# Six weight slots behind each layer's end taken by parts: first parts per half of the tokens, second parts last, GpSimd's rounding behind the norm

## The reference

```python
for i in range(2):                                   # first_block
    h = rms_norm(x, ln_mix_pre[i])
    m = gla_mixer(h, ...) if i == 0 else swa_sink_mixer(h, ...)
    x = x + rms_norm(m, ln_mix_post[i])
    h = rms_norm(x, ln_mlp_pre[i])
    f = jnp.square(jax.nn.relu(h @ w_up)) @ w_down
    x = x + rms_norm(f, ln_mlp_post[i])
for l in range(2):                                   # second_block
    h = even_mixer(x, ...) if l == 0 else odd_mixer(x, ...)
    x = layer_norm(ALPHA * x + h, ln_mix_g[l], ln_mix_b[l])
    x = layer_norm(ALPHA * x + swiglu(x, ...), ln_ffn_g[l], ln_ffn_b[l])
```

## Time and profile before

| | us |
|---|---|
| median of 3 runs | 2440.15 (2439.74 to 2441.57) |
| the profiled execution | 2440.48 |
| its span in the profile | 2438.6 |
| PE busy | 2380.8 (98% of the span) |
| POOL busy | 1095.1 (45%) |
| ACT busy | 933.6 (38%) |
| DVE busy | 706.0 (29%) |

### The profile page before, as it was taken

One profiled execution on the slowest core, in us unless ns is written; L12 is line 12 of the kernel. 1 busy time (PEld: TensorE's weight loads), 2 busy tenths in 40 slices (PEclk: granted clock), 3 DMA queues, 4 the chain that ended last, 5 costly groups with the idle time before them and its releaser, 6 DMA issues.

```text
span 2438.6 us, 29746 instructions
## 1 busy us (share of the span) xinstructions
PE 2380.8 (98%) x11723; PEld 1958.7 (80%) x11723; DVE 706.0 (29%) x1160; ACT 933.6 (38%) x1872; POOL 1095.1 (45%) x899
## 2 busy tenths in 40 slices
PE   8999999999989999999999999999999999999998
PEld 7867888888867888887887788888888768888887
DVE  2223430122454420223254541101152374110103
ACT  4523442433474442433254423323333572332331
POOL 4523544454433554444354444444445503444443
PEclk9999999999999999999999999999999999999999
DMA  5312233332312333322231233333333302333332
GB/s 177 87 51 67 87 96 98 93 100 82 87 35 70 94 97 96 97 97 82 83 108 61 69 96 104 97 96 97 100 95 82 96 1 80 116 100 95 95 100 74
DMA packets 161330, 215.59 MB, mean 88 GB/s; under 512 B 38175, under 2 KB 86039, under 8 KB 161191
## 3 DMA queue, kind: packets, MB, share of 16 engines
q1 hardware_dynamic: 157632, 203.65, 27.8%
q10 hardware_dynamic: 3559, 10.04, 1.2%
HBM read 211.00 MB, written 2.10 MB: 87 GB/s over the span
## 4 chain that ended last, share of the span: by engine, by line
PE 91%; DVE 5%; POOL 2%; issue 1%; ACT 1%; DMA 0%; ACTq 0%; DVEq 0%; POOLq 0%
PE PS L333 15%; PE PS L334 14%; PE PS L335 14%; PE PS L339 13%; PE PS L341 13%; PE PS L340 13%; PE PS L1393 1%; PE PS L1375 1%; PE PS L414 1%; PE PS L2191 1%; POOL WL L306 1%; DVE X L654 1%; PE PS L993 1%; PE PS L2178 0%; DVE X L536 0%
## 5 line engine op out<-in xcount | busy, mean ns | idle before, releaser
L306 POOL TENSOR_TENSOR WL<-WS,WH 128x512 fp32r<-128x512 f32 (+2 forms) x788 | 1005.4, 1283 | 1132.0 <-ACT WH L299 1127.8
L299 ACT ACTIVATE WH<-WS 128x512 fp32r<-128x512 f32 (+2 forms) x788 | 479.5, 615 | 1240.5 <-PE PS L341 626.7
L333 PE MATMUL PS<-AH,WH 128*128 128x512 f32 (+1 forms) x1712 | 641.0, 374 | 4.4 <-DVE AL L449 3.2
L334 PE MATMUL PS<-AL,WH 128*128 128x512 f32 (+1 forms) x1712 | 637.8, 373 | 0.0
L335 PE MATMUL PS<-AH,WL 128*128 128x512 f32 (+1 forms) x1712 | 637.7, 372 | 0.0
L333 PEld LDWEIGHTS PS<-AH,WH 128*128 128x128 f32 x1712 | 324.9, 190 | 62.7 <-issue 5.4
L335 PEld LDWEIGHTS PS<-AH,WL 128*128 128x128 f32 x1712 | 324.8, 190 | 56.0
L334 PEld LDWEIGHTS PS<-AL,WH 128*128 128x128 f32 x1712 | 324.9, 190 | 55.4 <-issue 0.5
L341 PE MATMUL PS<-WH,h_HL 128*128 128x512 f32 x864 | 336.1, 389 | 0.0
L339 PE MATMUL PS<-WH,h_HH 128*128 128x512 f32 x864 | 336.1, 389 | 0.0
L340 PE MATMUL PS<-WL,h_HH 128*128 128x512 f32 x864 | 336.1, 389 | 0.0
(11 more groups left out here) (320 smaller groups left out, 1887.5 us busy)
## 6 DMA issues: line engine op xcount, KB each, us to landing
WS<-in_mlp_w_up_dram SPq DMA_DIRECT2D x128, 256.0 KB, 2.8
WS<-in_mlp_w_down_dram SPq DMA_DIRECT2D x128, 256.0 KB, 2.6
WS<-in_ffn_w_gate_dram SPq DMA_DIRECT2D x176, 128.0 KB, 2.1
WS<-in_ffn_w_up_dram SPq DMA_DIRECT2D x176, 128.0 KB, 2.2
WS<-in_ffn_w_down_dram SPq DMA_DIRECT2D x88, 256.0 KB, 2.6
WS<-in_gla_w_in_dram SPq DMA_DIRECT2D x48, 256.0 KB, 2.7
WS<-in_even_w_in_dram SPq DMA_DIRECT2D x48, 256.0 KB, 2.7
WS<-in_odd_w_in_dram SPq DMA_DIRECT2D x32, 256.0 KB, 2.7
```

The source lines that it names most:

```text
L299: e.activation(WH[:, s, 0:n], WS[:, s, 0:n], ACT.Copy).then_inc(hi.sem, hi.tick(i))
L306: e.tensor_tensor(WL[:, s, 0:n], WS[:, s, 0:n], WH[:, s, 0:n].bitcast(F32), ALU.subtract).then_inc(lo.sem, lo.tick(i))
L333: e.matmul(o, h, xh[:, cs], start=start, stop=False, skip_group_check=free)
L334: e.matmul(o, h, xl[:, cs], start=False, stop=False, skip_group_check=free)
```

## The change

In a head PE now takes first parts of the weights only, for pieces 0 to 3 and then 4 and 5: all matmuls `AH` by `WH`, then all `AL` by `WH`. The transposes of the second half stand between the halves. The matmuls with `WL` follow behind both halves, all tokens at once. POOL makes the six second parts behind the last tile's norm, for which it waits. ACT and DVE take the features of the first half one bank at a time between their other work. The layer norm's variance of tile 3 is taken ahead of the features.

```diff
-                for half in range(2):
-                    for kc in range(HEAD):
-                        if half == 0 and kc == HEAD - 1:
-                            head()
-                        w.wait_ge(lo, i0 + kc)
-                        for at in ready(kc, half):
-                            w.wait_ge(*at)
...
-                            q = three(kc, m, cs)
-                        if half == 1:
-                            q.then_inc(mm.sem, mm.tick("used", i0 + kc))
+                for half in range(2):
+                    if half:
+                        head()
+                    cs = slice(256 * half, 256 * half + 256) if kind == "F" else slice(0, T)
+                    ms = range(count(0)) if kind == "F" else (2 * half, 2 * half + 1)
+                    for kcs in (range(HEAD - 2), range(HEAD - 2, HEAD)):
+                        for kc in kcs:
+                            w.wait_ge(hi, i0 + kc)
+                            for at in ready(kc, half, False):
+                                w.wait_ge(*at)
+                            for m in ms:
...
+                                one(kc, m, WH, xs[kc][0], cs, start=kc == 0 and (kind == "T" or half == 0))
+                        for kc in kcs:
+                            for at in ready(kc, half):
+                                w.wait_ge(*at)
+                            for m in ms:
+                                one(kc, m, WH, xs[kc][1], cs)
+                for kc in range(HEAD):
+                    w.wait_ge(lo, i0 + kc)
+                    for m in range(count(kc)):
+                        q = one(kc, m, WL, xs[kc][0])
+                    q.then_inc(mm.sem, mm.tick("used", i0 + kc))
@@ act_rms_close
-            run(weight_steps(weight_hi, e, w, name + ".1", nk, nk - TAIL))
+            late = weight_steps(weight_hi, e, w, name + ".1", nk, nk - TAIL)
+            for _ in range(4):
+                next(late)
+            act_feat(e, w, name, 0, BA, gain, free, [0])
             act_put(e, w, name, 3, 1, BA[3], other)
-            act_feat(e, w, name, 0, BA, gain, free, range(2))
+            act_feat(e, w, name, 0, BA, gain, free, [1])
             sumsq(2)
-            act_feat(e, w, name, 0, BA, gain, free, range(2, 4))
             sumsq(3)
+            next(late)
+            act_feat(e, w, name, 0, BA, gain, free, [2])
+            run(late)
+            act_feat(e, w, name, 0, BA, gain, free, [3])
@@ dve_rms_close
-            dve_feat(e, w, name, 0, BA, gain, free, range(2))
+            dve_feat(e, w, name, 0, BA, gain, free, [0])
             dve_add(e, w, name, 3)
-            dve_feat(e, w, name, 0, BA, gain, free, range(2, 4))
+            dve_feat(e, w, name, 0, BA, gain, free, [1])
             if normed:
                 dve_norm_mid(e, w, name, 2)
                 dve_norm_out(e, w, name, 2)
                 dve_norm_mid(e, w, name, 3)
                 dve_norm_out(e, w, name, 3)
+            dve_feat(e, w, name, 0, BA, gain, free, range(2, 4))
@@ pool_rms_close
-            late = weight_steps(weight_lo, e, w, name + ".1", nk, nk - TAIL)
-            for _ in range(3):
-                next(late)
             pool_rstd(e, w, name, 3)
-            next(late)
             if normed:
                 pool_norm_mid(e, w, name, 2)
-            run(late)
-            if normed:
                 pool_norm_mid(e, w, name, 3)
+            w.wait_ge(ve, "hn" if normed else "x", name, 3)
+            run(weight_steps(weight_lo, e, w, name + ".1", nk, nk - TAIL))
@@ dve_ln_close
             dve_ln_put(e, w, name, 3, 1, b1[3], scale)
+            dve_ln_var(e, w, name, 3)
             if not last:
-                dve_feat(e, w, name, 0, b1, None, free)
+                dve_feat(e, w, name, 0, b1, None, free, range(2))
             dve_ln_out(e, w, name, 2, b_)
-            dve_ln_mean(e, w, name, 3, g, gtok)
+            dve_ln_centre(e, w, name, 3, g, gtok)
+            if not last:
+                dve_feat(e, w, name, 0, b1, None, free, [2])
             dve_ln_out(e, w, name, 3, b_)
+            if not last:
+                dve_feat(e, w, name, 0, b1, None, free, [3])
@@ pool_ln_close
-            for t in range(3):
+            for t in range(4):
                 pool_ln_rstd(e, w, name, t)
-            late = weight_steps(weight_lo, e, w, name + ".1", nk, nk - TAIL)
-            for _ in range(5):
-                next(late)
-            pool_ln_rstd(e, w, name, 3)
-            run(late)
+            w.wait_ge(ve, "x", name, 3)
+            run(weight_steps(weight_lo, e, w, name + ".1", nk, nk - TAIL))
```

More of the change, by code:

```diff
@@ L324, in gemm, with one, three @@
             i0 = first[name]
-            def three(kc, m, cs=slice(0, T)):
-                s, n, (xh, xl), b = (i0 + kc) % NS, width(i0 + kc), xs[kc], banks[m]
-                last, start = kc == nk - 1, kc == 0 and cs.start == 0
-                free = head is not None
+            def one(kc, m, weight, x, cs=slice(0, T), start=False, stop=False):
+                s, n, b = (i0 + kc) % NS, width(i0 + kc), banks[m]
                 if kind == "F":
-                    h, l = WH[:, s, m * mw:(m + 1) * mw], WL[:, s, m * mw:(m + 1) * mw]
-                    o = PS[b][0:mw, cs]
-                    e.matmul(o, h, xh[:, cs], start=start, stop=False, skip_group_check=free)
-                    e.matmul(o, h, xl[:, cs], start=False, stop=False, skip_group_check=free)
-                    return e.matmul(o, l, xh[:, cs], start=False, stop=last, skip_group_check=free)
-                h, l = WH[:, s, 0:n], WL[:, s, 0:n]
-                o = PS[b][:, 0:n]
-                ts = slice(m * P, (m + 1) * P)
-                e.matmul(o, xh[:, ts], h, start=start, stop=False, skip_group_check=free)
-                e.matmul(o, xh[:, ts], l, start=False, stop=False, skip_group_check=free)
-                return e.matmul(o, xl[:, ts], h, start=False, stop=last, skip_group_check=free)
+                    return e.matmul(PS[b][0:mw, cs], weight[:, s, m * mw:(m + 1) * mw], x[:, cs], start=start, stop=stop,
+                                    skip_group_check=head is not None)
+                return e.matmul(PS[b][:, 0:n], x[:, m * P:(m + 1) * P], weight[:, s, 0:n], start=start, stop=stop,
+                                skip_group_check=head is not None)
+            def three(kc, m):
+                xh, xl = xs[kc]
+                one(kc, m, WH, xh, start=kc == 0)
+                if kind == "F":
+                    one(kc, m, WH, xl)
+                    return one(kc, m, WL, xh, stop=kc == nk - 1)
+                one(kc, m, WL, xh)
+                return one(kc, m, WH, xl, stop=kc == nk - 1)
             def count(kc):
@@ L350, in gemm @@
                 for half in range(2):
-                    for kc in range(HEAD):
-                        if half == 0 and kc == HEAD - 1:
-                            head()
-                        w.wait_ge(lo, i0 + kc)
-                        for at in ready(kc, half):
-                            w.wait_ge(*at)
-                        ms = range(count(kc)) if kind == "F" else (2 * half, 2 * half + 1)
-                        for m in ms:
-                            if kc == 0 and held.get(banks[m]):
-                                w.wait_ge(*held[banks[m]])
-                            cs = slice(256 * half, 256 * half + 256) if kind == "F" else slice(0, T)
-                            q = three(kc, m, cs)
-                        if half == 1:
-                            q.then_inc(mm.sem, mm.tick("used", i0 + kc))
+                    if half:
[8 more added lines that the diff above has]
+                            for m in ms:
+                                if kc == 0 and held.get(banks[m]):
+                                    w.wait_ge(*held[banks[m]])
+                                one(kc, m, WH, xs[kc][0], cs, start=kc == 0 and (kind == "T" or half == 0))
[9 more added lines that the diff above has]
+                    q.then_inc(mm.sem, mm.tick("used", i0 + kc))
                 yield HEAD - 1
@@ L453, in feats @@
         def feats(name):
-            return lambda kc, half: [(ve, "feat", name, half, kc)]
+            return lambda kc, half, rest=True: [(ve, "feat", name, half, kc) if rest else (sc, "feat", name, half, kc // 2)]
         def act_sumsq(e, w, name, t):
@@ L1249, in pool_gla @@
                 pool_norm_mid(e, w, "n0", t)
+            for t in range(2, 4):
+                pool_norm_mid(e, w, "n0", t)
+            w.wait_ge(ve, "hn", "n0", 3)
             for i in range(NS):
                 weight_lo(e, w, i)
-            for t in range(2, 4):
-                pool_norm_mid(e, w, "n0", t)
             run(weight_steps(weight_lo, e, w, "gla.q", 8))
```

25 lines of the change are left out of this document (17 added, 8 removed).

## The result

| | before, us | changed, us |
|---|---|---|
| median | 2440.82 (2439.74 to 2441.57, 4 runs) | 2422.40 (2419.45 to 2424.84, 4 runs) |
| ratio | | 0.9924, 95% interval 0.9907 to 0.9942 |
| span of the profiled execution | 2438.6 | 2423.0 |

The change takes 18.4 us off the median (0.76%); the forecast was 18.1, at 2422.0. The changed kernel was timed again in three later experiments: 2422.53, 2420.90 and 2421.63, ratios 0.9925, 0.9911 and 0.9925, each with an interval of some 0.0013 to either side.

The account below looks back on a forecast made before the run. PE, busy 98% of the span, bounds the kernel, with idle time to win only at layers' ends behind DVE's norms and features. Nine heads' wins sum to 18.1 us: 2440.15 - 18.1 = 2422.0, forecast range 2417 to 2427.

Parts of the forecast that it names:

- the sum: All nine heads: wins from earlier second transposes, less what goes behind them, add up to 18.1 us.
- swa.q0 and mlp1: Heads behind mlp0 and at mlp1: second transposes at 9.9 instead of 14.6 at swa.q0; wins 3.6 and 3.3 us.
- What is paid behind the second transposes: Every head: matmuls moved behind cost 1.1 us in kind F, 1.4 in kind T, 0.8 at odd.
- mlp0: Head at mlp0: transposes end 4.3 behind the last matmul, half done at 11.4; win 1.9 us.
- ev.u, ffn0, ffn1: Heads at these layers: earlier second transposes, less what goes behind; wins 3.9, 2.1 and 2.1 us.
- gla.q and gla.out.0: gla.q's second transposes about 20.5 instead of 22.55, win 1.0 us; gla.out.0's features in time anyway, 0.2.
- odd: Odd layer's head: tile 3 written no earlier than 1804.0, 1804.83 before; 0.8 us won goes behind, win 0.
- The first (the clock stays): Heads mlp0, swa.q0, mlp1, ev.u: half clock again at all four shrinks the win by 6.8, to 2429; chance 0.17.
- The second (the norm isn't earlier): Layers' ends: DVE's own chain keeps the last norm late, seven heads pay 7.8 us, 2448; chance 0.05.
- the fourth: Heads and elsewhere: features quicker by 1 us a head and clock drops elsewhere go, 2414; chance 0.08.
- The third (ACT's order holds bank 2): Root-mean-square heads: ACT's new order delays bank 2, they win half, 5 us less, with clock drops, 2432; chance 0.12.
- The burst: POOL behind tile 3's scaling: six second weight parts take 7.7 us, hidden from PE at both ends.

Follow-up runs that it names:

- tiny: Kernel before, orders unchanged, with POOL's late second weight parts one column wide and the other columns' product left out; 2425.19 us, ratio 0.9931.
- no_wait: Changed kernel without POOL's wait for the last tile's norm, its roundings starting right behind the last power; 2432.84 us, ratio 0.9973.
- the fourth profile: Changed kernel profiled and timed once more with no edit, the last of its repeats; 2421.63 us, ratio 0.9925.
- square_first: Changed kernel with bank 2's features ahead of tile 3's square and scaling, and at gla.out's end ACT's square of tile 3 before bank 0's features; 2419.46 us.
- bank2: Changed kernel with both feature parts of bank 2 ahead of tile 3's square and scaling at root-mean-square ends; 2419.10 us, again 2419.26 us.
- narrow: Changed kernel with the WL matmuls in kind F heads as 48 of 256 columns instead of 24 of 512; 2424.20 us, ratio 0.9933.
- pe_old: Changed kernel with only PE's order in the heads back, all three matmuls of a piece together in each half; 2483.37 us, ratio 1.0167.

## Why the prediction was right

**The bound.** Right. The win lies where PE stood idle behind a layer's end, and a quiet POOL brings it (`tiny`, 17 us; `no_wait`, 10 us given back for one overlap at each end).

**The total.** That the median meets the forecast within 0.4 us is in part luck. Where no head behind a layer's end or gla.out.0 ran at half clock (the fourth profile), the heads win 20.2 us, 2.1 more than the sum; in the other three half clock at gla.out.0, mlp0 or odd takes it to 16.5, 18.9 and 18.2. The sum had neither, and the two happen to cancel.

**swa.q0 and mlp1.** Right nearly step by step: transposes done 2.1 behind the last matmul (2.3 in the sum), ACT's bank 2 at 7.1 (7.5), DVE's at 8.7 (9.0), second transposes at 9.8 (9.9). The wins are 3.6 and 3.6 (3.6 and 3.3). The waits inside the half are 1.2 us; the prediction calls them 1.6, while its own steps add up to 1.8 (0.1, 1.2 and 0.5).

**What is paid behind the second transposes.** From them to the seventh piece PE takes 11.81 us before and 12.97 after at swa.q0, and 11.30 and 12.71 at ev.u: 1.16 and 1.41, where 1.1 and 1.4 stood in the sum.

**mlp0.** 2.5 (2.0 with a stretch at half clock) against 1.9. Its own step was right: transposes done 4.2 behind the last matmul (4.3). The half was done at 11.0 instead of 11.4, and what holds it is found by `square_first`.

**ev.u, ffn0, ffn1.** 3.7 against 3.9, and 2.4 twice against 2.1: the half at ffn0 was 0.4 quicker than my chain on DVE, since nothing on it was late and PE alone set the time.

**gla.q and gla.out.0.** 1.2 to 1.4 (0.7 once) against 1.0, and 0.4 against 0.2; in one profile of four gla.out.0 lost 1.3, all clock.

**odd: the step that failed.** The sum had 0. Its mechanism was right: the second transposes came 7.5 behind the first instead of 8.6, and 0.8 was paid behind. With the clock at full that leaves a win of 0.4 (15.70). But in three of four profiles the head is 1.2 to 1.3 us longer than before. PE's timeline there and its windows, in the changed kernel:

```profile
1786.62 0.82 PE L332 MATMUL PS<-WH,AL 128*128 128x296 f32 x4 [1.63 <-DVE AL L452]
...
1787.81 3.38 PE L424 MATMUL PS<-CK,X 128*128 128x128 f32 x15 [0.27 <-DVE X L669]
```

```profile
1784.20:1787.50 3.30, 1.67 (x11) 1.21 (x9) 3.30 (x4) 0.00 (x0) 0.00 (x0) 1.00 0.27 110
1787.60:1790.90 3.30, 3.09 (x15) 3.09 (x16) 2.12 (x4) 1.64 (x3) 3.06 (x4) 0.50 0.28 57
```

The fifteen transposes take 3.38 us instead of 1.86. PE had been busy for 1.67 of the 3.30 us before it fell to 1.2 GHz. In the version bank2 the same two stretches read:

```profile
1784.26:1787.56 3.30, 1.66 (x11) 1.19 (x9) 3.30 (x4) 0.00 (x0) 0.00 (x0) 1.00 0.25 100
1787.66:1790.96 3.30, 3.08 (x26) 3.09 (x27) 2.63 (x6) 2.07 (x4) 3.06 (x4) 1.00 0.26 57
```

The same wait in the same place, and the clock stays at full. Eight profiles have this wait of 1.6 us in an unchanged odd head (the four of the changed kernel, two of `bank2`, `narrow` and `square_first`), and half clock follows in five. The kernel before was busy for even less of the time ahead of its second transposes there, and kept the full clock:

```profile
1801.50:1804.80 3.30, 1.47 (x11) 1.20 (x10) 3.10 (x3) 0.00 (x0) 1.93 (x2) 1.00 0.75 257
```

So half clock can follow such a wait and need not; what decides, no row shows. I had written of four heads (mlp0, swa.q0, mlp1, ev.u) that could keep it, and left out the one where my own chain had DVE late.

**The rivals.** The first (the clock stays) was wrong in place: swa.q0, mlp1 and ev.u are free of it in all four profiles, mlp0 in three; half clock turned up at the odd head instead. The second (the norm isn't earlier) and the fourth fell. The third (ACT's order holds bank 2) is there, but as the 0.7 us a head that my own chain contained; the rest of it would need 5. Its 2432 was also too high by its own terms: 5 us and two stretches of 1.7 give 2430.

**POOL, and who waits.** The burst took 7.5 (7.7). PE waits in no head for a second part. Nothing of SP's queue or the seventh piece shows in PE's timeline.

## What to carry to other kernels

When a helper engine's bulk work runs beside a chain of small steps that the main engine waits for, price both things that it does, the stretching of the neighbour and the place in its own queue, and move it where nobody waits; then give the main engine an order in which the bulk result is wanted last. The parts hang together: with only POOL's part taken back the kernel was 23 us slower than before, with only PE's 41. And after each such gain look once more at what stands in front of a work item that needs nothing but finished data.

## What the runs showed of the hardware that I had not expected

The same code with the same wait of 1.6 us ran at half clock in three of four profiles and at full clock in the fourth: beyond its own length that wait cost either nothing or about 1.6 us (15.70 against 17.25). One profile does not settle whether a short wait costs the clock.

The clock also falls with no wait near. Some 34 us behind the fall at the odd head it falls again in the first three profiles of the changed kernel, though PE was busy for all of the stretch before (2.3 us of it with 20 matmuls of 8 columns):

```profile
1818.30:1821.60 3.30, 3.30 (x26) 3.10 (x26) 0.19 (x1) 1.26 (x2) 2.64 (x3) 1.00 0.24 78
1821.80:1825.00 3.20, 3.20 (x9) 2.35 (x8) 0.00 (x0) 0.00 (x0) 0.00 (x0) 0.50 0.31 82
```

In the eight profiles with the same odd head, this fall and the one at the odd head come together in five and are both missing in three. Why stays open. Long waits cost twice: the 7.35 us for which PE stood in `pe_old` were followed by matmuls of 256 columns 0.21 us apart, where 0.12 is usual.
